# All weight slots at one offset modulo 512 bytes, and 256-column products in the late FFN's input units

## What is computed

```python
def _swiglu(h, w_in, w_out):              # first block, two per layer, 2 layers, D_FF = 2816
    a, b = jnp.split(h @ w_in, 2, axis=-1)
    return (jax.nn.silu(a) * b) @ w_out
...
def swiglu(h, w_gu, w_down):              # second block, one per layer, 4 layers, D_FF_2 = 2816
    gate, up = jnp.split(h @ w_gu, 2, axis=-1)
    return (jax.nn.silu(gate) * up) @ w_down
...
for i in range(DEPTH_2):                  # second block
    ...
    x = x + mix
    x = x + mem_cross_attention(rmsnorm(x, norm_cross[i]), mem_n, ca_w_q[i], ca_w_kv[i], ca_w_o[i])
    x = x + swiglu(rmsnorm(x, norm_ffn[i]), ffn_w_gu[i], ffn_w_down[i])
return rmsnorm(x, norm_final)
```

## Time and profile before

| | |
|---|---|
| median of 3 runs | 2876.81 us (2873.92 to 2881.87) |
| the profiled execution | 2870.35 us |
| its span, first to last instruction | 2868.6 us |
| mean granted clock of TensorE | 0.976 |
| PE busy | 2717.4 us, 95% of the span, 21031 matmuls |
| DVE busy | 1940.6 us, 68% |
| ACT busy | 1389.5 us, 48% |
| HBM traffic | 530.7 MB, 185 GB/s over the span |

### The profile page before, as it was taken

One profiled execution on the slowest core, in us unless ns is written; L12 is line 12 of the kernel. 1 busy time (PEld: TensorE's weight loads), 2 busy tenths in 40 slices (PEclk: granted clock), 3 DMA queues, 4 the chain that ended last, 5 costly groups with the idle time before them and its releaser, 6 DMA issues.

```text
span 2868.6 us, 50786 instructions
## 1 busy us (share of the span) xinstructions
PE 2717.4 (95%) x21031; PEld 2579.0 (90%) x21031; DVE 1940.6 (68%) x2727; ACT 1389.5 (48%) x1664; POOL 0.7 (0%) x5
## 2 busy tenths in 40 slices
PE   6799979999999699999999999999999999999998
PEld 6799959999999599999989989989999899999897
DVE  5787786878877755576566776566665566775665
ACT  3333634435446354465554536554554544655544
POOL 0000000000000000000000000000000000000000
PEclk8899979999999899999999999999999999999999
DMA  8988505987985045654355643445665355643553
GB/s 232 307 292 265 176 30 185 299 293 257 295 276 177 15 165 187 206 189 153 114 176 184 206 140 105 159 138 198 207 197 171 108 200 195 206 147 114 177 187 106
DMA packets 458800, 533.03 MB, mean 186 GB/s; under 512 B 9879, under 2 KB 435081, under 8 KB 458633
## 3 DMA queue, kind: packets, MB, share of 16 engines
q1 hardware_dynamic: 457340, 530.11, 56.6%
q10 hardware_dynamic: 1293, 0.65, 0.1%
HBM read 528.10 MB, written 2.62 MB: 185 GB/s over the span
## 4 chain that ended last, share of the span: by engine, by line
PE 83%; DVE 9%; ACT 3%; issue 3%; DMA 2%; SPq 1%; ACTq 0%; DVEq 0%
PE ps L2097 14%; PE ps L2082 11%; PE ps L1930 9%; PE ps L2472 7%; PE ps L1912 7%; PE ps L1913 6%; PE ps L1914 6%; PE ps L2083 6%; DVE wlo L1206 2%; PE ps L2137 2%; DMA work<-in_ada_w 2%; DVE work L1586 2%; PE ps L2166 1%; PE ps L2282 1%; PE ps L2284 1%
## 5 line engine op out<-in xcount | busy, mean ns | idle before, releaser
L1206 DVE TENSOR_TENSOR wlo<-raw,whi 128x2048 fp32r<-128x2048 f32 (+1 forms) x514 | 976.0, 1920 | 383.2 <-ACT whi L774 383.0
L774 ACT ACTIVATE whi<-raw 128x2048 fp32r<-128x2048 f32 (+1 forms) x514 | 826.1, 1614 | 332.3 <-PE ps L1914 89.3
L2082 PE MATMUL ps<-parts_f,whi 128*128 128x512 f32 x1408 | 497.7, 396 | 11.9 <-issue 11.9
L1912 PE MATMUL ps<-hhi,whi 128*128 128x256 f32 x1600 | 451.6, 282 | 16.7 <-issue 14.0
L1913 PE MATMUL ps<-hlo,whi 128*128 128x256 f32 x1600 | 445.2, 278 | 0.0
L1914 PE MATMUL ps<-hhi,wlo 128*128 128x256 f32 x1600 | 444.7, 278 | 0.0
L2083 PE MATMUL ps<-parts_f,wlo 128*128 128x256 f32 x1408 | 396.2, 281 | 0.0
L2097 PE MATMUL ps<-ghi,whi 128*128 128x256 f32 x1280 | 356.2, 278 | 6.4 <-DVE wlo L1206 6.4
L2097 PE MATMUL ps<-glo,whi 128*128 128x256 f32 x1280 | 356.3, 278 | 0.0
L2097 PE MATMUL ps<-ghi,wlo 128*128 128x256 f32 x1280 | 355.7, 278 | 0.0
L2082 PEld LDWEIGHTS ps<-parts_f,whi 128*128 128x128 f32 x1408 | 266.0, 189 | 72.5 <-issue 13.9
(11 more groups left out here) (275 smaller groups left out, 4588.6 us busy)
## 6 DMA issues: line engine op xcount, KB each, us to landing
raw<-in_ffn_w_in SPq DMA_DIRECT2D x88, 1024.0 KB, 10.5
raw<-in_ffn_w_gu SPq DMA_DIRECT2D x88, 1024.0 KB, 5.1
work<-in_ada_w SPq DMA_DIRECT2D x72, 1024.0 KB, 8.8
raw<-in_ffn_w_out SPq DMA_DIRECT2D x88, 512.0 KB, 5.9
raw<-in_ffn_w_down SPq DMA_DIRECT2D x88, 512.0 KB, 5.6
raw<-in_ca_w_kv SPq DMA_DIRECT2D x32, 1024.0 KB, 5.8
raw<-in_mix_w_in SPq DMA_DIRECT2D x24, 1024.0 KB, 6.0
raw<-in_da_w_in SPq DMA_DIRECT2D x24, 1024.0 KB, 6.0
```

Of the source, the lines that this page charges most:

```text
L774: f(whi[:, s, 0:size], raw[:, s, 0:size], ACT.Copy).then_inc(hi_done[s], 1)
L1206: tt(wlo[:, s, 0:size], raw[:, s, 0:size], whi[:, s, 0:size].bitcast(F32), ALU.subtract).then_inc(lo_done[s], 1)
L1912: mm(dst, wh, xh, start=first, stop=False)
L2082: mm(ps[:, banks[m], :], th[:, k, c], parts_f[:, :, k, :], start=k == 0, stop=False)
```

## The change

It does two things.

1. The class `Slots` goes: `whi` and `wlo` are plain tensors of four slots, 64 floats less in all, and `phase_h` is 64 floats longer. In bytes modulo 512, counted from `whi`, all high and low weights of all slots now stand at 0; `hhi`, `hlo` stand at 448 and `mhi`, `mlo`, `ghi`, `glo`, `parts_f` at 64, as before.
2. `ab_wide` goes. The late input units use `ab` with `fhi`, `flo`: three 256-column matmuls for a tile, into one bank for A and one for B. ACT's two copies out of PSUM and DVE's two additions fall away; silu reads what DVE's first multiplication leaves, and the product is read from PSUM.

```diff
-class Slots:
-    def __getitem__(self, key):
-        rows, s, cols = key
-        at = UNIT * s + 32 * (s // 2)
-        return self.v[rows, at + cols.start:at + cols.stop]
...
-        whi = Slots(sb("whi", [P, SLOTS * UNIT + 32], F32R))
-        wlo = Slots(sb("wlo", [P, SLOTS * UNIT + 32], F32R))
+        whi = sb("whi", [P, SLOTS, UNIT], F32R)
+        wlo = sb("wlo", [P, SLOTS, UNIT], F32R)
         x = sb("x", [P, KT, S])
-        sb("phase_h", [P, 48])
+        sb("phase_h", [P, 112])
...
@@ ACT, ffn
                     if st.defer is not None:
-                        act.wait_ge(used[A], st.uses[A] + j + 1)
-                        if n:
-                            act.wait_ge(q["ffn_prod"], n)
-                        f(silu_a, ps[:, banks_a, S:], ACT.Copy).then_inc(q["wide_a"], 1)
-                        act.wait_ge(q["ffn_a"], n + 1)
+                        act.wait_ge(read[A], st.reads[A] + j + 1)
                         f(silu_a, silu_a, ACT.Silu).then_inc(q["ffn_silu"], 1)
...
-                    if st.defer is not None:
-                        act.wait_ge(used[B], st.uses[B] + j + 1)
-                        act.wait_ge(q["ffn_lo"], lo0 + j)
-                        f(product, ps[:, banks_b, S:], ACT.Copy).then_inc(q["wide_b"], 1)
...
@@ DVE, ffn
-                        dve.wait_ge(q["wide_a"], n + 1)
-                        tt(silu_a, ps[:, banks_a, 0:S], silu_a, ALU.add).then_inc(read[A], 1)
-                        dve.wait_ge(read[A], st.reads[A] + j + 1)
-                        tt(silu_a, silu_a, root, ALU.mult).then_inc(q["ffn_a"], 1)
+                        if st.reads[B] + j > 0:
+                            dve.wait_ge(read[B], st.reads[B] + j)
+                        tt(silu_a, rows2(ps[:, A, :]), root, ALU.mult).then_inc(read[A], 1)
                         ahead(pb)
                         dve.wait_ge(q["ffn_silu"], n + 1)
                         tt(silu_a, silu_a, root, ALU.mult).then_inc(q["ffn_sr"], 1)
-                        dve.wait_ge(q["wide_b"], n + 1)
-                        tt(product, ps[:, banks_b, 0:S], product, ALU.add).then_inc(read[B], 1)
-                        dve.wait_ge(read[B], st.reads[B] + j + 1)
+                        dve.wait_ge(used[B], st.uses[B] + j + 1)
                         dve.wait_ge(q["ffn_sr"], n + 1)
-                        tt(product, product, silu_a, ALU.mult).then_inc(q["ffn_prod"], 1)
+                        tt(product, rows2(ps[:, B, :]), silu_a, ALU.mult).then_inc(read[B], 1)
...
@@ PE, ffn, ab
+                    hi, lo = (hhi, hlo) if st.defer is None else (fhi, flo)
                     if first:
-                        both(slot, th, tl, st.h).then_inc(used[slot], 1)
+                        both(slot, th, tl, st.h, (hi, lo)).then_inc(used[slot], 1)
                         return
...
-                def ab_wide(slot, n, banks, first=False):
...
-                    for k, m in FIRST_ORDER if first and slot == A else TILE_ORDER:
-                        mm(ps[:, banks[m], :], th[:, k, c], parts_f[:, :, k, :], start=k == 0, stop=False)
-                        o = mm(ps[:, banks[m], 0:S], tl[:, k, c], fhi[:, k, :], start=False, stop=k == KT - 1)
```

More of the change, by code:

```diff
@@ L563, in tiles4 @@
             return v.rearrange("p (c t) -> p c t", t=cols)[:, keep, :]
-        def wide_banks(st):
-            A, B, O0, O1 = st.slots
-            return tuple(slice(min(n, m), max(n, m) + 1, abs(n - m)) for n, m in ((A, B), (O0, O1)))
         def ffn_pos(st, j):
@@ L587, in summed @@
             return 8 * (u if isinstance(u, int) and u <= ADA_BY_PE[0] else u - ADA_BY_PE[1] + ADA_BY_PE[0])
-        TILE_ORDER = [(k, m) for m in range(2) for k in range(KT)]
-        FIRST_ORDER = [(k, m) for k in range(KT) for m in range(2)]
         SG_V = SG_T = 4
@@ L880, in ffn @@
                     act.wait_ge(read[B], st.reads[B] + j + 1)
-                    if st.defer is not None:
-                        act.wait_ge(q["ffn_prod"], STEPS * st.defer + j + 1)
                     if st.uses[O1] + j > 0:
@@ L1392, in ffn @@
                     if st.defer is not None:
-                        banks_a, banks_b = wide_banks(st)
+                        n = STEPS * st.defer + j
                         dve.wait_ge(used[A], st.uses[A] + j + 1)
@@ L2064, in ab @@
                             c = slice(P * m, P * m + P)
-                            o = product(ps[:, slot, 256 * m:256 * m + 256], (th[:, k, c], tl[:, k, c]), hhi[:, k, :],
-                                        hlo[:, k, :], k == 0, k == KT - 1)
-                    o.then_inc(used[slot], 1)
-                def ab_wide(slot, n, banks, first=False):
-                    weights_of(slot, n)
-                    if first:
-                        for b in banks:
-                            pe.wait_ge(read[b], R[b])
-                    else:
-                        pe.wait_ge(read[slot], R[slot] + n)
-                    th, tl = tiles(slot)
-                    for k, m in FIRST_ORDER if first and slot == A else TILE_ORDER:
-                        if first and slot == A and m == 0:
-                            pe.wait_ge(q["norm_lo"], 8 * st.h + k + 1)
-                        c = slice(P * m, P * m + P)
-                        mm(ps[:, banks[m], :], th[:, k, c], parts_f[:, :, k, :], start=k == 0, stop=False)
-                        o = mm(ps[:, banks[m], 0:S], tl[:, k, c], fhi[:, k, :], start=False, stop=k == KT - 1)
+                            o = product(ps[:, slot, 256 * m:256 * m + 256], (th[:, k, c], tl[:, k, c]), hi[:, k, :],
+                                        lo[:, k, :], k == 0, k == KT - 1)
                     o.then_inc(used[slot], 1)
@@ L2099, in outs @@
                         o.then_inc(used[slot], 1)
+                ab(A, 0, first=True)
                 if st.defer is not None:
-                    ab_wide(A, 0, sorted((A, B)), first=True)
                     norm(st.late, True)
-                    ab_wide(B, 0, sorted((O0, O1)), first=True)
-                else:
-                    ab(A, 0, first=True)
-                    ab(B, 0)
+                ab(B, 0)
                 def step(n, first=False):
-                    if st.defer is not None:
-                        ab_wide(A, n + 1, sorted((A, B)))
-                        ab_wide(B, n + 1, sorted((O0, O1)))
-                    else:
-                        ab(A, n + 1)
-                        ab(B, n + 1)
+                    ab(A, n + 1)
+                    ab(B, n + 1)
                     outs(n, first)
```

13 lines of the change are left out of this document (4 added, 9 removed).

## The result

| | before | changed |
|---|---|---|
| median of 5 runs | 2875.71 us (2873.92 to 2881.87) | 2896.53 us (2889.72 to 2902.0) |
| the profiled execution, its span | 2870.35, 2868.6 us | 2897.67, 2895.9 us |

The ratio is 1.0067 [1.0047, 1.0087]: slower by 21 us, where a gain of 17 us was forecast. It lies beyond the range; of the rivals it is "the new places slow other streams", though not at its price.

What follows compares the result with a forecast made beforehand. It took PE's row of matmuls plus its few holes to bound the kernel. Matmuls -12.0 us and start -4.9 us make -16.9 us, from a median of 2876.8 to 2860 us; range 2849 to 2869 us.

Steps and rivals of the forecast that it cites:

- the new places slow other streams: Rival: weights at one residue put output units of all eight FFNs at the slow pace; 2907 us, chance 0.05.
- Part 4: Places modulo 512 of weights and columns in all units: taken as 0, with -3 us as the fast end.
- All weights at one residue: Same rival as "the new places slow other streams": +25 us in output units on top of +5; 2907 us, chance 0.05.
- Part 1: Late FFN input units: three narrow matmuls replace the wide tile, 0.20 or 0.10 us less a unit; -12.0 us.
- The rival that the late input units take the slow pace: Late input units' narrow matmuls run at 120 ns, turning the matmul gain into +10 us; 2882 us, chance 0.10.
- the Trainium skill's rule: A warm matmul costs N / 2.4 + about 2.5 ns, so narrow late tiles give +3.5 us in place of -12.0.
- Part 2: Start of each late FFN: shorter PE holes before A(1) and B(1), 0.7 us each; -4.9 us in all.
- its second term: Hole before B(1) at a late FFN's start: one DVE operation fewer, -0.7 us, counted in three of four FFNs.
- Part 3: Steady state of late steps: one DVE operation and two ACT copies fewer, hidden behind PE's matmuls; 0 us.

Runs made afterwards that it cites:

- e2: The kernel before with only the new places of weights and columns, wide tiles kept; 2899.5 us, ratio 1.0089.
- m1: Bare narrow matmul streams, not the reference's work, at 64 places of low weights and columns, four passes, two with other engines beside; 113.3 to 120.0 ns a matmul.
- e4: The changed kernel with columns moved to 192 and 320 modulo 512, all weights still at one place; 2891.3 us, ratio 1.0062.
- e6: The changed kernel with low weights 256 bytes above the high ones, columns as in it; 2893.6 us, ratio 1.0069.
- e1: The changed kernel with the old places (class Slots back), so narrow tiles and the new start remain; 2850.4 us, ratio 0.9923.
- e10: The kernel before, wide tiles and late start kept, with low weights 128 and all columns 192 above the high weights; 2869.3 us, ratio 1.0004.
- e9: The changed kernel with low weights 128 and all columns 192 above the high weights; 2848.2 us, ratio 0.9927.
- e8: The changed kernel with all columns 64 bytes below the weights, high and low weights at one place; 2871.7 us, ratio 1.0015.
- m2: Bare streams again: 16 places in four matmul orders, then 24 pairs of places, at once or after a 0.5 us hole; wide tile 353.2 ns at (0, 64).
- e3: The changed kernel with low weights 128 bytes above the high ones, columns as in it; 2880.8 us, ratio 1.003.
- e5: The changed kernel with low weights 128 above the high ones, columns at 320 and 448 modulo 512; 2851.7 us, ratio 0.9926.

## Why the prediction was wrong

**Part 4, the places modulo 512, which it put at 0 ("I take 0"), is the step that failed.** The places alone cost 24 us with wide tiles (`e2`) and 46 us with the narrow ones. The two paces were seen, but only in the second early FFN's slot 1, and read as an oddity of a pair that the change removes. The trace held more: token-major units at 117.8 ns throughout, several units of `hhi` and `mhi` at that pace. I asked how many matmuls are slow now; the question was which relation of places each stream gets, and whether any stream had shown a pace at that relation. For (0, 64) none had, since high and low weights never stood at one place before. That was a reason to keep a wide range: the rival's price, 2907 us, was outside it at a chance of 0.05.

**"All weights at one residue" was the right rival.** Its cause was half right: the weights at one place with columns 64 above them is a slow place (`m1`, with the exceptions above), but columns 320 or low weights 256 above are the same place modulo 256 (`e4`, `e6`). The argument against it, that slots 0 and 1 had high weights 64 below the columns at the fast pace, fell because the low weights' place counts as well. Its price, 2907 us, was too high by 11 us only, and that is in part luck. It asked +25 us of the output units and +10 of the late input units against the kernel before. By the sum over all units the output units gave +14.0 and the late input units +4.7 (17.9 less 13.2), and +15.3 came from `hhi` and `mhi` streams, which it did not count. The slow pace there is 4.5 ns a matmul above the fast one (117.8 less 113.3), not 6; rows 8 are another place, (128, 64), whose slow pace is 118.9.

**Part 1, matmuls, -12.0 us:** right at the old places and 0.0 at the new ones. The 12.0 us of `e1` (3.9 + 2.1 + 4.0 + 2.0) are those of 18 of the 20 units that the forecast counts, for which it had 10.8, so that the sums agree to the tenth is chance. The step that failed in it is the carrying over of 113 ns from the earlier trace rows, measured at the old places. The rival that the late input units take the slow pace came true beside the other, with three matmuls at 353 ns where it had put 358. By the Trainium skill's rule ("TensorE: Matmul & The Clock Gate", section "Wait — 56ns, not 53.3ns?") the estimates are 325.0 and 327.5 ns. The bare streams disagree with both: they have 340.3 to 353.3 for a wide tile and 340 to 360 for three narrow ones, by the place. What a matmul costs over its columns (256 at 2.4 GHz are 106.7 ns) is here 6.6 ns at a fast place and 11 to 13 at a slow one, so a fixed 2.5 ns agrees with neither.

**Part 2, the start, -4.9 us:** near in sum, mis-sized in its second term. The holes before A(1) add up to 5.95 us over the four late FFNs (1.48 and three times 1.49), before to 9.19 (2.25, 2.35, 2.25, 2.34): 3.2 us, forecast 2.8. Those before B(1) gave 0.56, 0.37 and 0.34 us in the first, third and fourth, less than the 0.7 each, and one of 0.54 us appeared in the second: 0.7 us, forecast 2.1. That is 4.0 us. The clock did not fall at the second late FFN as it had in the earlier trace rows, which gives back up to 1.7 us more. In `e1` the sum is seen as a whole: of the 20.0 us between the spans 2.7 were there before the last early FFN (code that the change doesn't touch), 12.0 lie within the late FFNs, and 5.3 are left.

**Part 3, DVE and ACT, 0:** right. No PE wait on either has appeared within the steps. One detail was misread and cost nothing: DVE's first operation (L1402) is already the one that frees A's banks in the kernel before, not its second.

With the places left out of the change, the forecast of 2860 us would have been 10 us too high (`e1` has 2850.4). The sum of the terms, 17 us, stands against 20 between the two profiled executions. The medians are 25 apart: executions of the kernel before, and of `e10`, also come at 2874 to 2882 us with a mean granted clock of 0.968 to 0.973, where `e1` had 0.976 to 0.979 in all four. One part of it stands in the traces. In the three wide kernels 5 of the 12 holes of 2.25 to 2.35 us at the start of a late FFN are followed within 1.5 us by a stretch of 3.4 us at half clock; in the nine narrow ones none of the 36 holes of 1.43 to 1.69 us is. But four such stretches, one at each late FFN, cost at most 7 us, and `e9` has a mean clock of 0.972 to 0.977 at 2847 to 2851 us, so the rest stays open.

## What to carry to other kernels

A matmul's cost is a matter of where its operands stand in a partition, too. Before a change that moves tensors, even by padding, write down for each stream where low weights and columns stand above the high weights, modulo 256 bytes, and look whether the trace shows a stream at each of the new pairs; where none does, the range has to hold the slow pace over all its matmuls (here 4.5 ns of 113). The duration column tells the pace at a glance (276 against 280 ns). A small kernel of bare streams gave in one run a table that seven versions of the whole had not. But give it the holes and the neighbours that the real one has: without them it missed the second pace of (0, 192), which cost the forecast of `e8`, and that of (0, 64).

## What the runs showed of the hardware

- 256-column `F32R` matmuls, each with its own 128-column weight load, have a few discrete paces at clock 1.00: 113.3 ns, 115.6 ns and some from 117.8 to 120 ns. Which one depends in the first place on where the low weights and the columns stand against the high weights, modulo 256 bytes, and not on DMAs, ACT or DVE (`m1`).
- At three of the four places tried in pairs, (128, 64), (0, 192) and (0, 64), two paces are stable: a stream of a whole stage can keep either (157.9 and 152.0 us in `e8` at one place). In `m2` the pace after a change of places went by what ran before, and after a hole of 0.5 us it was at times the other one. Only (128, 192) stood at 113.3 ns every time.
- The runs spread from 2868 to 2895 us in `e3` (10 runs) and from 2868 to 2888 in `e8` (10), whose output units have such a place in all slots, against 4 us in `e9` and in `e1` (4 runs each) and 6 in `e5`. The changed kernel, `e4` and `e6` spread by 9 to 14 us. That whole stages at one or the other pace make this spread was not shown: each kernel has one trace.
- Orders differ. The token-major order never went below 116.7 ns at 15 of the 16 places of `m2`, (128, 192) among them; at (0, 64) it had 117.8 upward and 113.5 downward. The wide tile is fastest at (64, 64), 340.3 to 340.6 ns, which is as good as three narrow ones; no version of the kernel with that place was run.
- What in the machine counts modulo 256 bytes stays open. The runs show the table, not its cause.
